# State-space mix of a hybrid trunk: the last convolution tile before the first keys, turned tiles copied out earlier, the spread of states moved in the second layer

## What is computed

```python
def _ssd_prep(p, conv_w, conv_b, dt_bias, pos):
    z, xbc, dt_raw = jnp.split(p, [MIX_WIDTH, MIX_WIDTH + SSD_CONV_DIM], axis=-1)
    xbc = jax.nn.silu(dwconv_centred(xbc, conv_w, conv_b))       # 5 taps, 2048 channels
    xs, bm, cm = jnp.split(xbc, [...], axis=-1)                   # 1024 of x, 512 of B, 512 of C
    if pos is not None:
        bm, cm = rope_2d(bm, *pos), rope_2d(cm, *pos)
    dt = jax.nn.softplus(dt_raw + dt_bias)

# per direction, in chunks of 128 tokens, for each of 4 groups of 4 heads of 64:
acs = jnp.cumsum(dA)                                              # dA = dt * a
L = jnp.exp(where(lower, acs_l - acs_s, -inf))
y_diag = einsum(C B^T, L, X)                                      # within a chunk
chunk_states = einsum(B, exp(acs_end - acs), X)                   # "keys" times B
h = h * exp(acs_end) + chunk_state                                # from chunk to chunk
y_off = einsum(C, h_in, exp(acs))                                 # from earlier chunks
y = y_diag + y_off + d_skip * xs
```

## Time and profile before

| | us |
|---|---|
| median of 3 runs | 3590.16 |
| lowest and highest run | 3574.8, 3593.56 |
| profiled execution, its own time | 3584.78 |
| its span, first to last instruction | 3583.0 |
| mean granted TensorE clock, share of full speed | 0.971 |

### The profile page before, as it was taken

The page is one execution under the profiler, slowest core; times in us unless marked ns, Lnnn a source line. Parts: engine busy times, 40 slices in busy tenths (PEclk is TensorE's granted clock), DMA queues, the critical chain, the costliest instruction groups (busy, mean ns, idle before and its releaser), DMA issues. The chain is left out here.

```text
span 3583.0 us, 72004 instructions
## 1 busy us (share of the span) xinstructions
PE 3261.5 (91%) x31390; PEld 1782.9 (50%) x31390; DVE 1663.3 (46%) x3252; ACT 1090.7 (30%) x1956; POOL 383.6 (11%) x349
## 2 busy tenths in 40 slices
PE   6989999999998899999998797998988887899997
PEld 3454444644565565443332345656755555674333
DVE  3584901764777873220000356833257777531111
ACT  2221101703666752121111321103145666420001
POOL 0051200311010100010000013112011010000000
PEclk8999999999999999999999799999999999999999
DMA  5103622162111111379998111834211111269996
GB/s 209 47 24 112 205 71 87 47 220 58 28 29 36 29 35 54 134 298 420 407 384 332 67 57 39 269 114 110 72 51 29 36 29 30 61 264 382 424 424 274
DMA packets 255436, 537.18 MB, mean 150 GB/s; under 512 B 49520, under 2 KB 173696, under 8 KB 222224
## 3 DMA queue, kind: packets, MB, share of 16 engines
q1 hardware_dynamic: 236064, 463.82, 35.5%
q0 software_dynamic: 19056, 68.69, 5.5%
HBM read 514.59 MB, written 17.87 MB: 149 GB/s over the span
## 5 line engine op out<-in xcount | busy, mean ns | idle before, releaser
L1295 PE MATMUL banks<-sb_h,sb_ring 128*128 128x512 f32 (+1 forms) x1344 | 474.8, 512 | 10.4 <-DMA sb_ring<-w_branch 6.7
L1295 PEld LDWEIGHTS banks<-sb_h,sb_ring 128*128 128x128 f32 x1344 | 254.3, 190 | 224.1 <-issue 195.8
L1832 PE MATMUL banks<-sb_h,sb_ring 128*128 128x512 f32 (+1 forms) x672 | 312.9, 591 | 6.2 <-DMA sb_ring<-w_in 4.2
L815 PE MATMUL banks<-sb_h,sb_ring 128*128 128x512 f32 x512 | 230.9, 609 | 19.4 <-SPq L237 19.4
L1823 PE MATMUL banks<-inv 64*64 64x64 f32 x4864 | 141.8, 233 | 52.9 <-ACT inv L2257 35.3
L1832 PEld LDWEIGHTS banks<-sb_h,sb_ring 128*128 128x128 f32 x672 | 119.7, 194 | 123.1 <-issue 109.7
L3376 DVE TENSOR_TENSOR hrow<-hrow,banks 128x256 f32<-128x256 f32 x36 | 15.1, 421 | 355.9 <-ACT hrow L3412 355.9
L1823 PEld LDWEIGHTS banks<-inv 64*64 64x64 f32 x4864 | 123.0, 146 | 112.5 <-issue 111.8
L1295 PE MATMUL banks<-sb_branch,sb_ring 128*128 128x512 f32 (+1 forms) x512 | 170.9, 487 | 0.0
L3224 PE MATMUL banks<-gu,xs 128*64 128x512 f32 x768 | 168.4, 594 | 1.8 <-DMA gu<-gu_pairs 1.3
L815 PEld LDWEIGHTS banks<-sb_h,sb_ring 128*128 128x128 f32 x512 | 99.3, 196 | 138.2 <-issue 117.5
(11 more groups left out here) (501 smaller groups left out, 5592.9 us busy)
## 6 DMA issues: line engine op xcount, KB each, us to landing
gu<-gu_pairs SPq DMA_DIRECT2D x64, 1536.0 KB, 16.6
gu<-gu_tiles SPq DMA_DIRECT2D x57, 1024.0 KB, 9.4
sb_ring<-w_in SPq DMA_DIRECT2D x24, 2048.0 KB, 9.2
sb_ring<-gu_tiles SPq DMA_DIRECT2D x39, 1024.0 KB, 9.5
vtok<-w_mod POOLq DMA_DIRECT2D x64, 512.0 KB, 5.5
sb_ring<-down_pairs SPq DMA_DIRECT2D x32, 1024.0 KB, 14.0
sb_ring<-w_in SPq DMA_DIRECT2D x58, 512.0 KB, 3.9
sb_ring<-down_tiles SPq DMA_DIRECT2D x25, 1024.0 KB, 8.0
```

What stands on the lines that cost most here:

```text
L815: m = mm(k.bank[j], k.ring[:, h, kt, P * j:P * j + P], k.h[:, kt], start=kt == 0, stop=kt == KT - 1)
L1295: mm = nc.tensor.matmul(out, left(kt), right(kt), start=kt == 0, stop=kt == KT - 1)
L1832: m = mm(k.bank[banks[j]][:, WHOLE[j]:], w[:, j, kt], k.h[:, kt, WHOLE[j]:], start=kt == 0, stop=kt == KT - 1)
```

## The change

ACT's list in both layers: the copies of turned tiles go in front of `filtered(n-1)`, and the first three (`take_b(0)`, `take_b(1)`, `take_x(0)`) one tile earlier. In the turns n of 12 and 13 it is `take_b(0)` and `take_b(1)`, in 14 and 15 `take_x(0)` and `take_x(1)`; `take_x(2)` stays behind the loop. DVE's list in both layers: `keyed(0)`, with its wait for four copied tiles of x, stood in front of `taps(15)` and now stands behind it. DVE's list in the second layer alone (`per == 2`): `spread(g+1)` stood at the end of a group's second unit, behind `skipped` and `added`, and now stands directly behind that unit's `weighted`. PE's and POOL's lists and all transfers stay as they are.

```diff
@@ ssd_mix, block.scalar
             for n in range(16):
                 convolved(n)
+                if n in (12, 13):
+                    take_b(n - 12)
+                if n in (14, 15):
+                    take_x(n - 14)
                 if n:
                     filtered(n - 1)
...
-                if n == 13:
-                    take_b(0)
-                if n == 14:
-                    take_b(1)
-                if n == 15:
-                    take_x(0)
-                    take_x(1)
-                    take_x(2)
+            take_x(2)
             take_x(3)
@@ ssd_mix, block.vector
             for n in range(16):
-                if n == 15:
-                    v.wait_ge(s.xtok, 4)
-                    keyed(0)
                 taps(n)
...
+            v.wait_ge(s.xtok, 4)
+            keyed(0)
             spread(0)
             reads(0)
...
                     weighted(u)
+                    if per == 2 and u % per == 1 and g + 1 < GROUPS:
+                        spread(g + 1)
                     if u + 1 < NU:
                         reads(u + 1)
                     scaled(u)
@@
                 if u < NU:
                     added(u)
-                    if u % per == 1 and g + 1 < GROUPS:
+                    if per > 2 and u % per == 1 and g + 1 < GROUPS:
                         spread(g + 1)
```

## The result

The changed kernel takes 3561.5 us (median, 3557.8 to 3565.0), the kernel before 3588.0 us in the same measurement; the ratio is 0.9931, with an interval of 0.9902 to 0.9961. Measured once more (experiment e9_changed) it is 0.9926, interval 0.9914 to 0.9938: by this ratio 26.5 us less of 3583.2. The forecast was 3559 us, 25.7 us less than the profiled execution. The profiled executions' spans are 3583.0 and 3556.0 us, a difference of 27.0.

The account below looks back on a forecast made before the run. PE, busy 91% of the span, was taken as the bound, with time to win in its waits and slow work after them; 5.4 + 8.8 + 11.5 = 25.7 us off 3584.8 gave 3559 us, range 3545 to 3576.

Parts of the forecast that it names:

- Part 1: Convolution, both layers: ACT copies turned tiles one tile sooner, two PE waits of 1.35 us go; 2.7 us a layer, 5.4 us.
- Part 2: Behind the last convolution tile, both layers: last taps before the keys bring the first states sooner; 4.4 us a layer, 8.8 us.
- The undisturbed chain of 6.95 us: Last tile's end to PE's third state: ACT's copy, taps, first key, two state matmuls, ACT's first state, handover to PE.
- The two additions: Lengthening the chain to the third state: DVE and POOL obstructing each other, 2.6 us; state matmuls at half speed, 1.0 us.
- The upper end of 6.6 us a layer: Best case for the last taps before the keys: neither obstruction by POOL nor a slow stretch; 6.6 us a layer.
- Part 3: Second layer's loop: spread in front of reads fills DVE's idle time; 3.8 + 3.8 + 3.9 = 11.5 us.
- PE's floor as worked out: Second layer's loop: PE's pair of units without its 3.21 us wait and 1.7 us of clock loss, 12.5 us.
- rival A: Second layer's loop becomes DVE's: POOL's mk falls on spread and keys, pair stays near 16.5 us; 3568 us, chance 0.11.
- B: Convolution part keeps its length: turns wait for something else, or keys fall under mk and slow clock returns; 3567 us, chance 0.06.
- C: Slower: DVE and POOL exclude one another everywhere, the loop loses 4.3 us a pair, 13 in all; 3592 us, chance 0.02.
- D: Nothing to be seen: the reordered lists end at the same waits; 3585 us, chance 0.02.
- The rule of exclusion: At the keys: two-SBUF-input DVE and GpSimd instructions block each other; by it 2 us a layer, undisturbed 6.6.

Follow-up runs that it names:

- e9_changed: The changed kernel itself measured once more, on the same chip as the kernel with both further edits; 3554.6 us, ratio to the kernel before 0.9926.
- e5_pool: The changed kernel with POOL's first product xd of the loop made to wait until DVE has the three first keys; ratio to the kernel before 0.9918.
- e2_keys: The kernel before with only DVE's last taps put in front of the first keys, both layers; copies and spread as before; ratio 0.9975.
- e6_spread_both: The changed kernel with the spread directly behind weighted in the first layer too; ratio to the kernel before 0.9935.
- e1_copies: The kernel before with only ACT's copies of the turned tiles made sooner; keys and spread as before; ratio 0.9979.
- e4_fill: The kernel before with useless matmuls put into PE's waits, before the third state and, in the second layer's loop, before passed; ratio 0.9978.

## Why the prediction was right

**Part 1.** Forecast 2.7 us a layer, end 3.1; measured 3.1 (the tiles' spacing 9.28 to 7.74 us, twice). The rows' 1.35 us left out the handover around the wait. Alone the part is worth more, see below.

**Part 2.** Forecast 4.4 us a layer; from tile 15's start to the second segments it was 4.15 and 3.9. The chain to the third state was to be 10.6 us. The second state ended just before DVE's L1039 at 2149.65, which waited for it, so the third state ended the PE piece that began at 2147.82 and started about 10.8 us behind the last tile's end (2138.76). The undisturbed chain of 6.95 us stood: in e5_pool, where POOL is out of the way and the clock full, the second state ends just before 2145.89, and so the third starts about 7.2 us behind the tile's end (2138.64).

The two additions were each too small, and the number was met by luck. The obstruction was 0.7 us on the taps and 1.7 + 0.8 on the second key, 3.2 for an assumed 2.6, and the slow stretch cost 4.20 x 0.41 = 1.7 us for 1.0. With these the prediction's own sum would be 6.95 + 3.2 + 1.7 = 11.9. It was 10.8 because the path was another one. The sum led over ACT's copy of the first state, which was done at 2146.4, more than a microsecond before the second state began. The measured path leads over the second key and the second state. That path has some 0.4 us of slack where nothing disturbs it, and only about half of the slow stretch lies in front of the third state. The upper end of 6.6 us a layer left out the 2.5 us of clock that an undisturbed chain gives back as well: in e5_pool the stretch from tile 15 is 18.5 us, 8.7 and 8.4 less than in the kernel before.

**What the split does not say.** The terms 5.4 and 8.8 us hold for the two parts in company: the spacing gave 6.2 and the stretch behind the last tile 8.1. They are not what each part is worth alone. Alone the parts give 8.7 and 11.7 us in the two stretches, together 14.2. The 6.2 us between are found in two pieces. With both parts POOL's mk starts just when DVE wants the second key, PE waits 2.02 us, and the stretch from tile 15 takes 23.0 us for 21.2 in e2_keys: 2 x 1.8, nearly all of it slow clock (21.33 us in the second layer of e6_spread_both, with the same waits at full speed). And e1_copies alone shortens the tail behind the last tile (27.17 to 25.34 and 26.91 to 26.24 us), 2.5 us, of which 2 x 0.9 are the shorter wait in front of the turns and the rest is clock. So some 4 of the 6.2 us depend on where the clock fell in single executions. The prediction did not look for such an exchange between the two parts.

**Part 3.** Forecast 11.5 us, measured 12.2 in the changed kernel and 12.1 alone: 5.0 and 3.0 from the two full pairs and 4.2 from the third, for 3.8, 3.8 and 3.9. The pairs were to take 13.5 each; they took 12.4, PE's floor as worked out, and 14.3, where one mk of 2.81 us came between W and the spread. The clock was at 1.00, as forecast. Their mean, 13.4, is near the forecast's by luck: neither pair is of that length, and rival A's mechanism is what happened in the second of them. There the prediction's own sign against part 3 is seen, a PE wait in front of products (1.25 us). It had counted this wait as covered by some 2 us, and mk's hold on the spread (2.38 us for 0.68) used that up. The part gained all the same.

**Rivals.** A (3568) has its mechanism in the second pair, at 1.9 us and not in every pair. B (3567) falls in its first half, since the waits in front of the tiles went and did not come back elsewhere (e1_copies). Of its second half a part came true: mk lay on the second key and the slow clock came back, 1.7 us of it, and still the part gave 4.15 and 3.9 us. C (slower) would have needed a slow clock behind every obstruction; in the loop none came, and PE's longest wait there was 1.25 us. D is out. The rule of exclusion, set against part 2, is right, and took 3.2 us of DVE's time at this place; that the part still gained is because mk did not touch the first key (0.69 us, begun just before mk) and because the old chain had paid 3.1 us of it too.

## What to carry to other kernels

A work list is bound by the wait that ends last, and a wait can be worth itself plus the slow clock behind it; both stand in the trace, and a filler of useless matmuls in the wait tells them apart. The slow clock does not follow every time, so its share is not read from one execution alone. When DVE's rows are longer than their kind, look which POOL instruction with operands in SBUF lies beside them: making POOL wait (one line, no work moved) took 9 us out of the traced stretches here, a third of what the whole change brought. Edits that move triggers shift such meetings, so their gains need not add: those of the copies and the keys did not in the traces, those of e5_pool and e6_spread_both did.

## What the runs showed of the hardware that was not expected

- The same two waits of PE (0.83 or 0.84, and 2.02 us) were followed by a granted clock of 0.59 in one execution (3.49 us for eight state instructions) and by full speed in another (1.99 us). In e2_keys a wait of 3.21 us was followed by full speed (1.13 us for four instructions) and the next one of 3.21 us in the same loop by a clock of 0.62 (2.08 us). In e4_fill the clock fell to 0.61 behind waits of 1.78 and 0.29 us in the second layer, and not behind the same two in the first. In the loop it stayed at 1.00 behind 1.25 us.
- DVE and POOL held each other up in both directions: in the changed kernel POOL's mk took 2.36 and 2.81 us behind DVE's instructions for 1.90 alone, and DVE's key of 256 columns up to 2.12 for 0.42.
- Of two instructions of DVE on the same tile beside the same mk, the one with both inputs in SBUF was held up (1.48 us for 0.69) and the one that read a bank was not (0.69, e5_pool).
